# Sample state products of a hybrid decoder layer: high and low halves stacked on 128 rows in one fp32r matmul, in place of padded fp32

## The chip, the cores and the metric

The kernel runs on one core of one Trainium2 chip. The metric is the device time of one execution in microseconds (us). The engines are PE (TensorE: matmuls, and PEld, its weight loads), DVE (VectorE), ACT (ScalarE), POOL (GpSimd) and SP, which issues most of the DMAs.

## The reference, cut to what matters

One decoder layer serves 256 prompt tokens and a sample group of 8 sequences with 4 new tokens each (32 sample rows). Two recurrent branches update a 128x128 state for each sequence and head:

```python
# HGRN2, 16 heads
S = exp(G_last)[..., None] * S + einsum('bhsd,bhsv->bhdv', k * exp(G_last - G), i)
# gated delta rule, 32 value heads in 16 pairs
S = exp(g_last) * S + einsum('bhsd,bhsv->bhdv', k * exp(g_last - gam)[..., None], v_new)
```

The einsum over `s` (4 tokens for each sample sequence) is the "state product" that the change rewrites. Around it the layer does a large input projection, two output projections, a merge, and a feed-forward block.

## The kernel before

**Projections.** All dense products run on PE in `products` (L574 to L576). Weights arrive in pieces of 512 columns; ACT rounds each piece to fp32r (`whi`, L982), DVE takes the rest (`wlo`, L1429), and PE does three fp32r matmuls of 288 columns (256 prompt and 32 sample) for each 128-row block. A slab of 128 output columns is 48 such matmuls. Pieces are split three ahead of their use.

**Interleaving.** The recurrent work is written out by hand as steps `s` between the projection's matmuls: on PE there is a step before each 6 matmuls. An HGRN head spans 4 slabs (32 steps), a pair of delta heads 6 slabs (48 steps). Every engine walks the same step numbers in its own order and waits on counted semaphores; an engine that waits holds back all that stands behind it.

**HGRN state product of the sample** (head n). Step 0: PE transposes the 32 sample columns of decayed keys (`hX[:,3]`) and inputs (`hi_`) into bank 3 (L633, L634). Step 1: ACT copies them to `htoks` (L1070, semaphore `h_tok`); DVE masks scores into `hAT` (`h_at`). POOL then writes `hiX` (L2062, prompt) and `hiXs` (L2064): the 32 input rows repeated for 8 sequences and masked with `cm4`, 1024 columns (`h_spread`). Step 8: PE contracts `htok` with `hiX` (L643) and `htoks` with `hiXs` (L645), two 512-column matmuls each; rows 32 to 127 of the sample operands are zeros. Step 10: DVE adds the products to the states (L1574, L1578). Step 15: PE forms the outputs (L654 to L661).

**Delta state product of the sample** (pair n, e = 0, 1). Steps 42 to 44: PE transposes q, k, v (L707), ACT gets the norms, DVE scales q, k (`g_tokqk`) and v (L1704, `g_tokv`), then finishes the previous pair's output (L1792, L1794 `g_out`), which ACT rounds into `ohi` (L1243). POOL scales the keys by the decays (L2175: `gbek`, `gkl`, `gkls`), then issues the load of the next convolution rows (L2140). Step 0: PE transposes (L726), ACT copies (L1185 to L1190, `g_qpt`). Step 2: PE makes decay sums (L734, L735). Step 4: DVE makes `gA`, POOL the level masks (L2194), PE the halo transposes (L696); step 5: DVE does the gate product `gz` (L1721), the tap copies (L1656) and the halo copy (L1659); step 6: PE transposes level 0 (L753); step 7: DVE makes `gUi`, `gUs` (L1741, L1742); step 8: PE goes on (L765). Step 13: PE reads the old states; step 15: DVE makes `guTs`; step 16: PE transposes it; step 17: ACT copies `gvns` (L1216). POOL spreads it into `gvX` (L2225, once per e). Steps 20 and 24: PE contracts `gkls` with `gvX` (L817, two 512-column matmuls per step). Steps 21 and 25: DVE adds the product to the state (L1766).

## Time and profile before

| what | value |
|---|---|
| runs of the kernel before | 3898.64 us median of 3 (3895.19 to 3902.77) |
| profiled execution: its time | 3902.09 us |
| profiled execution: span, first to last instruction | 3900.6 us |
| PE busy | 3652.7 us (94%) |
| DVE, ACT, POOL busy | 2267.7, 1801.1, 869.9 us |
| mean granted TensorE clock | 0.956 of full speed |

A row of grouped instructions gives line, engine, operation, output and inputs, shapes and count, then busy us and mean ns of one. A matmul's modelled duration includes a tail that overlaps the next one, so the pace of PE is read from start to start. An fp32 matmul stands as two records.

### The profile page before, as it was taken

The numbers are of one execution on the slowest core, as the hardware profiler recorded it, in microseconds if no ns is written. First come the engines' busy times: TensorE is split into PE (matmuls) and PEld (weight loads), VectorE is DVE, ScalarE is ACT, GpSimd is POOL, SyncE is SP. The second block draws the span as 40 slices with busy tenths as digits, with TensorE's granted clock in tenths as the row PEclk, the third lists the DMA queues.
The fourth block names the chain that finished last, engine by engine and source line by source line (L and its number), as shares of the span: only waits on it lengthen the run. The fifth ranks groups of instructions, "written<-read, shape, count | busy, mean of one in ns | idle before, by whom it ended". The sixth has DMA issues, their size and how long they took to land.

```text
span 3900.6 us, 79284 instructions
## 1 busy us (share of the span) xinstructions
PE 3652.7 (94%) x25307; PEld 3326.0 (85%) x25307; DVE 2267.7 (58%) x4435; ACT 1801.1 (46%) x3802; POOL 869.9 (22%) x1035
## 2 busy tenths in 40 slices
PE   8799999999899999999999999999896999999997
PEld 1399999998888888888888988897685999999996
DVE  1466666646666656666566566545667545555555
ACT  1154544555454444445544454455463434444443
POOL 1022222211145444441244455411100000000000
PEclk9799999999999999999999999999997999999998
DMA  8454544568733333447634333357883555555553
GB/s 276 136 157 142 146 137 137 150 171 266 214 105 101 94 96 99 113 112 222 183 103 117 100 99 94 99 142 239 250 241 104 151 158 164 157 163 160 161 158 114
DMA packets 887591, 587.95 MB, mean 151 GB/s; under 512 B 23602, under 2 KB 820244, under 8 KB 886932
## 3 DMA queue, kind: packets, MB, share of 16 engines
q1 hardware_dynamic: 861268, 510.50, 45.6%
q0 software_dynamic: 26240, 76.41, 6.4%
q8 instruction: 43, 0.70, 0.1%
q14 instruction: 40, 0.33, 0.0%
...
## 4 chain that ended last, share of the span: by engine, by line
PE 80%; DVE 7%; issue 4%; ACT 3%; DMA 3%; POOL 1%; SPq 0%; DVEq 0%; ACTq 0%; POOLq 0%
PE acc L574 20%; PE acc L576 19%; PE acc L575 19%; PE acc L537 3%; PE bank L765 2%; PE bank L779 2%; PE bank L802 2%; PE bank L782 2%; PE bank L817 1%; DVE wlo L1429 1%; ACT whi L982 1%; PE bank L586 1%; DVE h_S L1574 1%; PE bank L587 1%; PE bank L661 1%
## 5 line engine op out<-in xcount | busy, mean ns | idle before, releaser
L1429 DVE TENSOR_TENSOR wlo<-raw,whi 128x512 fp32r<-128x512 f32 x1799 | 1266.5, 722 | 976.0 <-ACT whi L982 956.5
L982 ACT ACTIVATE whi<-raw 128x512 fp32r<-128x512 f32 x1799 | 1099.0, 628 | 992.4 <-PE acc L576 935.1
L574 PE MATMUL acc<-ahi,whi 128*128 128x288 f32 x4112 | 1305.2, 317 | 43.5 <-DVE wlo L1429 17.4
L575 PE MATMUL acc<-alo,whi 128*128 128x288 f32 x4112 | 1235.4, 300 | 0.0
L576 PE MATMUL acc<-ahi,wlo 128*128 128x288 f32 x4112 | 1231.1, 299 | 0.0
L574 PEld LDWEIGHTS acc<-ahi,whi 128*128 128x128 f32 x4112 | 793.9, 193 | 67.7 <-issue 41.0
L575 PEld LDWEIGHTS acc<-alo,whi 128*128 128x128 f32 x4112 | 795.4, 193 | 13.2 <-issue 11.5
L576 PEld LDWEIGHTS acc<-ahi,wlo 128*128 128x128 f32 x4112 | 795.1, 193 | 0.0
L574 PE MATMUL acc<-ohi,whi 128*128 128x288 f32 x1792 | 539.4, 301 | 26.1 <-DVE olo L1949 9.7
L575 PE MATMUL acc<-olo,whi 128*128 128x288 f32 x1792 | 534.0, 298 | 0.0
L576 PE MATMUL acc<-ohi,wlo 128*128 128x288 f32 x1792 | 532.3, 297 | 0.0
L574 PEld LDWEIGHTS acc<-ohi,whi 128*128 128x128 f32 x1792 | 340.9, 190 | 49.4 <-DVE wlo L1429 18.3
L575 PEld LDWEIGHTS acc<-olo,whi 128*128 128x128 f32 x1792 | 341.3, 190 | 2.4
L576 PEld LDWEIGHTS acc<-ohi,wlo 128*128 128x128 f32 x1792 | 342.3, 191 | 0.0
L1202 ACT ACTIVATE g_PU<-bank 128x512 f32<-128x512 f32 x80 | 47.8, 598 | 314.4 <-PE bank L765 239.2
L2194 POOL TENSOR_TENSOR g_lev<-g_A,levm 128x512 f32<-128x512 f32 x96 | 139.7, 1455 | 173.0 <-PE bank L765 114.4
L1752 DVE TENSOR_TENSOR g_Ui<-g_Ui,bank 128x512 f32<-128x512 f32 x80 | 54.7, 684 | 116.8 <-PE bank L782 111.6
L1672 DVE SCALAR_TENSOR_TENSOR g_ca<-g_U,g_cw,g_ca 128x312 f32<-128x312 f32 x192 | 118.0, 615 | 6.8
L537 PE MATMUL acc<-raw,cst 128*9 128x512 f32 x256 | 114.2, 601 | 8.0 <-DMA raw<-in_w_ada 8.0
L586 PE MATMUL bank<-whi,cs 128*18 128x512 f32 x256 | 101.3, 396 | 15.7 <-DVE wlo L1429 14.7
L765 PE MATMUL bank<-g_Ui,g_lev 128*128 128x128 f32 x640 | 88.1, 281 | 24.8 <-DVE g_Us L1742 22.1
L765 PEld LDWEIGHTS bank<-g_Ui,g_lev 128*128 128x128 f32 x640 | 78.7, 192 | 33.8 <-issue 33.7
...
## 6 DMA issues: line engine op xcount, KB each, us to landing
...
raw<-in_w_ada SPq DMA_DIRECT2D x192, 512.0 KB, 4.7
raw<-in_w_up SPq DMA_DIRECT2D x128, 512.0 KB, 4.1
raw<-in_w_down SPq DMA_DIRECT2D x128, 512.0 KB, 3.9
...
```

The costliest lines, as they stand in the source:

```text
L537: last = mm(acc[k][0:NC, :], cst[:, 2 * l + a, :], raw[:, 2 * (l % 4) + a].rearrange("p k c -> p (k c)"), start=(l + a == 0), stop=(l == 7 ...
L574: mm(bank[:, 0:T], whi[:, s, r, :], hi[:, kt, :], start=(kt == 0), stop=False, skip_group_check=True)
L575: mm(bank[:, 0:T], whi[:, s, r, :], lo[:, kt, :], start=False, stop=False, skip_group_check=True)
L576: last = mm(bank[:, 0:T], wlo[:, s, r, :], hi[:, kt, :], start=False, stop=(kt == KT - 1), skip_group_check=True)
L586: mm(R[4][0:2 * NC, :], cs2[:, kt, :], whi[:, s].rearrange("p k c -> p (k c)"), start=(kt == 0), stop=False)
L765: last = mm(R[3][:, p * P:(p + 1) * P], glev[:, l % 2, p, :], gUi[:, p, :], start=True, stop=True)
L779: last = mm(R[2][:, p * P:(p + 1) * P], gT[:, p, :], gPU[:, p, :], start=True, stop=True)
L782: last = mm(R[6][:, p * P:(p + 1) * P], gPU[:, p, :], gT[:, p, :], start=True, stop=True)
L982: f(whi[:, s], raw[:, r], ACT.Copy).then_inc(sg["hi_made"], 1)
L1429: tt_(wlo[:, s], raw[:, r], whi[:, s].bitcast(F32), SUB).then_inc(sg["lo_made"], 1)
L1672: stt(gca[:, 0:CW], gU[:, k, a:a + CW], gcw[:, k, a:a + 1], gca[:, 0:CW], MUL, ADD).then_inc(sg["g_part" if a < 3 else "g_tap"], 1)
L2194: last = pt(glev[:, l % 2], gA[:, :, :], levm[:, l, :].unsqueeze(1).to_broadcast([P, 4, P]), MUL)
```

## The change

The 32 sample rows of each state product are repeated four times along the partitions. One operand's four groups hold high, high, low, low (keys), the other's high, low, high, low (inputs or values), high being the fp32r rounding and low the rest. One fp32r matmul over 128 rows then sums all four cross products, in place of an fp32 matmul with 96 rows of zeros. To get there the transposes are fed with four copies (`hk4`, `hi4`, `gck4`, `guT4`), ACT rounds all rows, DVE overwrites the low groups with the difference, and POOL spreads 128 rows, with fp32r as output type. `gkls` leaves POOL; DVE makes `gk32` from bank 5 instead, and ACT and DVE split it at steps 4 and 5. Several of the new tiles lie in `gn1` and `gn2`, which are idle then. In the setup `cm4` becomes four stacked copies, and the strict mask of the sample is repeated for column 8 of `tab`.

```diff
-                htoks = sb("h_toks", [P, 2, P])
+                hvs = sb("h_vs", [P, P])
+                hst = sb("h_st", [P, 2, P], F32R)
+                hk4 = sb("h_k4", [P, 4, NS])
+                hi4 = sb("h_i4", [P, 4, NS])
                 hAT = sb("h_AT", [P, T])
                 hiX = sb("h_iX", [P, 2, 4, P])
-                hiXs = sb("h_iXs", [P, NB, P])
+                hiXs = sb("h_iXs", [P, NB, P], F32R)
...
-            gkls = sb("g_kls", [P, 2, P])
+            gkst = sb("g_kst", [P, 2, P], F32R)
...
+            gkhi = gn1[:, :, :].rearrange("p a t -> p (a t)")[:, 0:2 * P].rearrange("p (e d) -> p e d", d=P)
+            gvst = gn2[:, :, :].rearrange("p a t -> p (a t)")[:, 0:2 * P].rearrange("p (e v) -> p e v", v=P)
+            gck4 = gn2[:, :, :].rearrange("p a t -> p (a t)")[:, 2 * P:3 * P]
+            guT4 = gkhi.rearrange("p e (g b t) -> p e g b t", g=4, t=TS)
...
-                    turn(R[3][0:NS, 0:P], hX[:, 3, TP:T], ident[:, :])
-                    turn(R[3][0:NS, P:2 * P], hi_[:, TP:T], ident[:, :])
+                    turn(R[3][:, 0:P], hk4[:, :, :].rearrange("p g t -> p (g t)"), ident[:, :])
+                    turn(R[3][:, P:2 * P], hi4[:, :, :].rearrange("p g t -> p (g t)"), ident[:, :])
...
-                        last = mm(R[2 + a][:, :], htoks[:, 0, :], hiXs[:, 4 * a:4 * a + 4, :].rearrange("p c v -> p (c v)"),
+                        last = mm(R[2 + a][:, :], hst[:, 0, :], hiXs[:, 4 * a:4 * a + 4, :].rearrange("p c v -> p (c v)"),
...
-                    mm(R[7][:, TP:T], htoks[:, 1, :], hAT[:, TP:T], start=False, stop=False, skip_group_check=True)
+                    mm(R[7][:, TP:T], hvs[:, :], hAT[:, TP:T], start=False, stop=False, skip_group_check=True)
...
-                            last = turn(bank[0:m, k * P:(k + 1) * P], gC[:, k, a * P:a * P + m], ident[:, :])
+                            if (a, k) == (2, 1):
+                                turn(bank[:, k * P:(k + 1) * P], gck4, ident[:, :])
+                            else:
+                                last = turn(bank[0:m, k * P:(k + 1) * P], gC[:, k, a * P:a * P + m], ident[:, :])
...
-                        last = turn(R[5][0:NS, e * P:(e + 1) * P], guTs[:, e, :], ident[:, :])
+                        last = turn(R[5][:, e * P:(e + 1) * P], gkhi[:, e, :], ident[:, :])
...
                     pe.wait_ge(sg["g_vns"], n + 1)
+                    pe.wait_ge(sg["g_u1"], EARLIER + n + 1)
                     pe.wait_ge(sg["g_snew"], 2 * n + e)
                     for a in range(2):
-                        last = mm(R[4 + a][:, :], gkls[:, e, :], gvX[:, 4 * a:4 * a + 4, :].rearrange("p b v -> p (b v)"),
+                        last = mm(R[4 + a][:, :], gkst[:, e, :], gvX[:, 4 * a:4 * a + 4, :].rearrange("p b v -> p (b v)"),
...
                     act.wait_ge(sg["h_turned"], i)
+                    f(hi4[:, :, :], acc[at.bank(2)][:, TP:T].unsqueeze(1).to_broadcast([P, 4, NS]), ACT.Copy)
...
-                    f(htoks[0:NS, :, :], R[3][0:NS, 0:2 * P].rearrange("p (k d) -> p k d", d=P), ACT.Copy).then_inc(sg["h_tok"], 1)
+                    f(hvs[0:NS, :], R[3][0:NS, P:2 * P], ACT.Copy)
+                    f(hst[:, :, :], R[3][:, 0:2 * P].rearrange("p (k d) -> p k d", d=P), ACT.Copy).then_inc(sg["h_tok"], 1)
...
                 if s == 4:
+                    act.wait_ge(sg["g_tokv"], EARLIER + n + 1)
+                    f(gkhi[2 * NS:P].bitcast(F32R), gk32[2 * NS:P], ACT.Copy)
+                    f(gkst[0:2 * NS], gk32[0:2 * NS], ACT.Copy)
...
                     act.wait_ge(sg["g_vtt"], n + 1)
-                    f(gvns[0:NS, :, :], R[5][0:NS, 0:2 * P].rearrange("p (e v) -> p e v", v=P), ACT.Copy).then_inc(sg["g_vns"], 1)
+                    f(gvns[0:NS, :, :], R[5][0:NS, 0:2 * P].rearrange("p (e v) -> p e v", v=P), ACT.Copy)
+                    act.wait_ge(sg["g_olo"], n)
+                    f(gvst.bitcast(F32R), R[5][:, 0:2 * P].rearrange("p (e v) -> p e v", v=P), ACT.Copy).then_inc(sg["g_vns"], 1)
...
-                    tt_(hAT[0:NS, TP:T], R[4][0:NS, TP:T], smask[:, :], MUL).then_inc(sg["h_at"], 1)
+                    tt_(hAT[0:NS, TP:T], R[4][0:NS, TP:T], smask[:, :], MUL)
+                    dve.wait_ge(sg["h_tok"], n + 1)
+                    for rows_, k in ((slice(2 * NS, P), 0), (slice(NS, 2 * NS), 1), (slice(3 * NS, P), 1)):
+                        last = tt_(hst[rows_, k, :], R[3][rows_, k * P:(k + 1) * P], hst[rows_, k, :].bitcast(F32), SUB)
+                    last.then_inc(sg["h_at"], 1)
...
+                    if k == 1:
+                        tt_(gck4.rearrange("p (g b t) -> p g b t", g=4, t=TS),
+                            sample_of(gca[:, :], TS)[:, :, 0:TS].unsqueeze(1).to_broadcast([P, 4, NB, TS]),
+                            sample_of(gce[:, :], TS)[:, :, 0:TS].unsqueeze(1).to_broadcast([P, 4, NB, TS]), MUL)
...
-                            last = ts(gbv[0:m, a, e, :], bank[0:m, (2 + e) * P:(3 + e) * P], gsc[0:m, e, a:a + 1], None, MUL)
+                            ts(gbv[0:m, a, e, :], bank[0:m, (2 + e) * P:(3 + e) * P], gsc[0:m, e, a:a + 1], None, MUL)
+                    for e in range(2):
+                        last = ts(gk32[:, e, :], R[5][:, P:2 * P], gss[:, 2, 2, 1:2], gsc[:, e, 8:9], MUL, MUL)
...
+                    tt_(gkst[2 * NS:P], gk32[2 * NS:P], gkhi[2 * NS:P], SUB)
...
-                    tt_(guTs[:, :, :].rearrange("p e (b t) -> p e b t", t=TS), R[7][:, 64:128].rearrange("p (e b t) -> p e b t", e=2, t=TS),
-                        gqws[:, :, :, 1, :], ADD).then_inc(sg["g_vt"], 1)
+                    for e in range(2):
+                        last = tt_(guT4[:, e], R[7][:, 64 + e * NS:64 + (e + 1) * NS].rearrange("p (b t) -> p b t", t=TS).unsqueeze(1)
+                                   .to_broadcast([P, 4, NB, TS]), gqws[:, e, :, 1, :].unsqueeze(1).to_broadcast([P, 4, NB, TS]), ADD)
+                    last.then_inc(sg["g_vt"], 1)
+                if s == 17:
+                    dve.wait_ge(sg["g_vns"], n + 1)
+                    for rows_ in (slice(NS, 2 * NS), slice(3 * NS, P)):
+                        last = tt_(gvst[rows_], R[5][rows_, 0:2 * P].rearrange("p (e v) -> p e v", v=P), gvst[rows_], SUB)
+                    last.then_inc(sg["g_vlo"], 1)
...
-                pt(hiXs[0:NS, :, :], htoks[0:NS, 1, :].unsqueeze(1).to_broadcast([NS, NB, P]),
-                   cm4[:, :].unsqueeze(2).to_broadcast([NS, NB, P]), MUL).then_inc(sg["h_spread"], 1)
+                pool.wait_ge(sg["h_at"], n + 1)
+                pt(hiXs[:, :, :], hst[:, 1, :].bitcast(F32).unsqueeze(1).to_broadcast([P, NB, P]),
+                   cm4[:, :].unsqueeze(2).to_broadcast([P, NB, P]), MUL).then_inc(sg["h_spread"], 1)
...
-                pt(hX[:, 3, :], hk[:, :], hE[:, 3, :], MUL).then_inc(sg["h_decayed_p"], 1)
+                pt(hX[:, 3, :], hk[:, :], hE[:, 3, :], MUL)
+                pt(hk4[:, :, :], hk[:, TP:T].unsqueeze(1).to_broadcast([P, 4, NS]), hE[:, 3, TP:T].unsqueeze(1).to_broadcast([P, 4, NS]),
+                   MUL).then_inc(sg["h_decayed_p"], 1)
...
-                        scaled(gkl[:, a, c], P, a, 27 + 2 * a + c)
-                scaled(gkls[0:NS], NS, 2, 8).then_inc(sg["g_tokd"], 1)
+                        last = scaled(gkl[:, a, c], P, a, 27 + 2 * a + c)
+                last.then_inc(sg["g_tokd"], 1)
...
-                pool.wait_ge(sg["g_vns"], n + 1)
+                pool.wait_ge(sg["g_vlo"], EARLIER + n + 1)
...
-                    pt(gvX[0:NS, :, :], gvns[0:NS, e, :].unsqueeze(1).to_broadcast([NS, NB, P]),
-                       cm4[:, :].unsqueeze(2).to_broadcast([NS, NB, P]), MUL).then_inc(sg["g_vx"], 1)
+                    pt(gvX[:, :, :], gvst[:, e, :].unsqueeze(1).to_broadcast([P, NB, P]),
+                       cm4[:, :].unsqueeze(2).to_broadcast([P, NB, P]), MUL).then_inc(sg["g_vx"], 1)
```

## Rows read from the trace of the kernel before

**Rows 1.** The page: its header, busy time of PE, chain that ended last.

```profile
span 3900.6 us, 79284 instructions
PE 3652.7 (94%) x25307; PEld 3326.0 (85%) x25307; DVE 2267.7 (58%) x4435; ACT 1801.1 (46%) x3802; POOL 869.9 (22%) x1035
...
PE 80%; DVE 7%; issue 4%; ACT 3%; DMA 3%; POOL 1%; SPq 0%; DVEq 0%; ACTq 0%; POOLq 0%
```

**Rows 2.** Groups of instructions on PE, whole span.

```profile
L586 PE MATMUL bank<-whi,cs 128*18 128x512 f32 x256 | 101.3, 396 | 15.7 <-DVE wlo L1429 14.7
...
L817 PE MATMUL bank<-g_vX,g_kls 128*128 128x512 f32 x128 | 60.2, 592 | 0.0
...
L645 PE MATMUL bank<-h_iXs,h_toks 128*128 128x512 f32 x64 | 30.1, 592 | 0.0
```

**Rows 3.** Timeline of PE, HGRN step 8: start us, duration us, instruction.

```profile
222.10 1.88 PE L643 MATMUL bank<-h_iX,h_tok 128*128 128x512 f32 x4
223.82 1.88 PE L645 MATMUL bank<-h_iXs,h_toks 128*128 128x512 f32 x4
...
226.20 0.30 PE L576 MATMUL acc<-ahi,wlo 128*128 128x288 f32 x1
226.33 0.29 PE L574 MATMUL acc<-ahi,whi 128*128 128x288 f32 x1
```

**Rows 4.** Timeline of PE, HGRN step 0: transposes of 128 and 32 columns.

```profile
214.56 0.27 PE L632 MATMUL bank<-ident,h_i 128*128 128x128 f32 x1
214.66 0.27 PE L633 MATMUL bank<-ident,h_X 128*32 128x128 f32 x1
214.77 0.27 PE L634 MATMUL bank<-ident,h_i 128*32 128x128 f32 x1
```

**Rows 5.** Waits of PE, 1000 to 2740 us: total us, times, longest.

```profile
PE bank L765 <- DVE g_Us L1742: 22.1, 14, 3.1
PE bank L696 <- DMA g_cc<-in_cache_conv: 19.7, 13, 1.7
PE bank L734 <- ACT g_QW L1190: 12.2, 15, 1.2
```

**Rows 6.** Timeline of ACT and POOL, HGRN steps 1 to 8.

```profile
216.78 0.36 ACT L1070 ACTIVATE h_toks<-bank 32x256 f32<-32x256 f32 x1
...
219.22 2.34 POOL L2064 TENSOR_TENSOR h_iXs<-h_toks,cm 32x1024 f32<-32x1024 f32 x1
```

**Rows 7.** Groups on POOL, 1125 to 1750 us.

```profile
L2219 POOL TENSOR_TENSOR g_S<-g_S,g_sc 128x1024 f32<-128x1024 f32 x14 | 26.2, 1888 | 4.3 <-PE bank L802 3.8
```

**Rows 8.** Single HGRN heads (first three) and delta pairs: window, length, busy, PEclk.

```profile
223.82:261.04 37.22, 36.78 (x252) 34.37 (x251) 24.56 (x49) 18.09 (x39) 8.80 (x8) 0.95 0.50 144
...
410.00:446.00 36.00, 35.48 (x252) 32.87 (x251) 23.82 (x49) 18.05 (x38) 8.79 (x8) 1.00 0.51 148
...
705.50:744.30 38.80, 38.28 (x251) 35.88 (x250) 23.88 (x49) 18.14 (x37) 8.79 (x8) 0.91 0.47 137
...
1136.10:1222.10 86.00, 81.11 (x595) 75.75 (x594) 54.05 (x112) 40.15 (x101) 40.46 (x45) 0.96 0.37 101
...
1563.50:1646.50 83.00, 78.20 (x595) 72.63 (x594) 53.71 (x112) 40.20 (x101) 40.36 (x45) 1.00 0.38 104
```

**Rows 9.** Timelines of DVE, ACT and PE, delta step 44 to step 2.

```profile
1249.76 1.62 DVE L1704 TENSOR_SCALAR g_bv<-bank,g_sc 128x128 f32<-128x128 f32 x6
...
1252.74 1.06 DVE L1794 TENSOR_TENSOR g_n<-g_o,g_z 128x576 f32<-128x576 f32 x1
...
1253.93 0.69 ACT L1243 ACTIVATE ohi<-g_n 128x576 f32 x1
...
1256.62 0.70 PE L734 MATMUL bank<-g_GR,m_incl 128*128 128x256 f32 x2 [0.83 <-ACT g_QW L1190]
```

**Rows 10.** Timelines of POOL and DVE, delta steps 4 and 5.

```profile
1262.18 2.47 POOL L2194 TENSOR_TENSOR g_lev<-g_A,levm 128x512 f32<-128x512 f32 x1 [2.90 <-DVE g_As L1732]
...
1263.04 0.44 DVE L1721 TENSOR_TENSOR g_z<-g_ca,g_ce 128x288 f32<-128x288 f32 x1
1263.40 4.32 DVE L1656 COPY g_cw<-vec 128x4 f32 x3
```

**Rows 11.** Timelines of POOL and PE, delta steps 17 to 20.

```profile
1292.54 2.01 POOL L2225 TENSOR_TENSOR g_vX<-g_vns,cm 32x1024 f32<-32x1024 f32 x1 [0.90 <-ACT g_vns L1216]
...
1299.05 1.45 PE L817 MATMUL bank<-g_vX,g_kls 128*128 128x512 f32 x3
```

More of the change, by code:

```diff
@@ L234, in hybrid_layer @@
             cm32 = sb("cm32", [P, P // HC])
+            cm4w = sb("cm4w", [P, 4 * NB])
+            mstr4 = sb("mstr4", [NS, P])
             lbt = sb("lbt", [P, HH, 2])
@@ L315, in hybrid_layer @@
                 gto = scoped(rows_out)("g_to", [27, 4, P])
-            gvX = sb("g_vX", [P, NB, P])
+                gk32 = scoped(rows_out)("g_k32", [P, 2, P])
+            gvX = sb("g_vX", [P, NB, P], F32R)
             gS = sb("g_S", [P, 4, 2, P])
@@ L1016, in _ @@
             f(bgs[:, 0:128], R[5][:, 0:128], ACT.Exp)
-            f(bgs[0:NS, 128:192], R[5][0:NS, 128:192], ACT.Exp)
+            f(bgs[0:NS, 128:160], R[5][0:NS, 128:160], ACT.Exp)
+            f(bgs[:, 160:192], R[5][:, 160:192], ACT.Exp)
             f(bgs[:, 192:576], R[3][:, 0:384], ACT.Exp).then_inc(sg["chunk_exp"], 1)
@@ L1487, in _ @@
             for b in range(NB):
-                last = ts(gxs[:, b, :], bgT[0:NS, 2, GH:2 * GH], cm4[:, b:b + 1], None, MUL)
+                last = ts(gxs[:, b, :], bgT[0:NS, 2, GH:2 * GH], cm4[0:NS, b:b + 1], None, MUL)
+            last = copy(mstr4[:, :].rearrange("p (g t) -> p g t", t=NS), m_str_s[:, :].unsqueeze(1).to_broadcast([NS, 4, NS]))
             last.then_inc(sg["bg_taken"], 1)
@@ L1497, in _ @@
                 for k in range(2):
-                    copy(tab[0:m, :, 3 + 3 * k + a], sums[:, k])
+                    copy(tab[0:m, :, 3 + 3 * k + a], sums[:, k]) if (a, k) != (2, 1) else copy(tab[:, :, 8], bgs[:, 160:192])
                 for c in range(2 if a < 2 else 0):
@@ L1504, in _ @@
             for rows_ in (slice(NS, 2 * NS), slice(2 * NS, P)):
-                nc.vector.memset(hiXs[rows_, :, :], 0.0)
                 nc.vector.memset(hAT[rows_, TP:T], 0.0)
-                last = nc.vector.memset(htoks[rows_, :, :], 0.0)
+                last = nc.vector.memset(hvs[rows_, :], 0.0)
             last.then_inc(sg["tab_made"], 1)
@@ L1634, in _ @@
             for rows_ in (slice(NS, 2 * NS), slice(2 * NS, P)):
-                nc.vector.memset(gvX[rows_, :, :], 0.0)
-                nc.vector.memset(gkls[rows_, :, :], 0.0)
                 nc.vector.memset(gvns[rows_, :, :], 0.0)
@@ L2017, in _ @@
                                     pattern=[[-1, P]], channel_multiplier=1).then_inc(sg["consts_made"], 1)
-            for t in (hmask, smask, reset, cm32, cm4, cm64, m_incl, m_str, m_str_s):
+            for t in (hmask, smask, reset, cm32, cm4w, cm64, m_incl, m_str, m_str_s):
                 nc.gpsimd.memset(t[:, :], 1.0)
@@ L2031, in _ @@
                 keep(chunked(t, n_, m), [[m, n_], [0, m]], m - 1, -1)
-            for t, n_, m in ((cm32, P // HC, HC), (cm4, NB, TS), (cm64, 2, GC)):
+            for t, n_, m in ((cm32, P // HC, HC), (cm4w, 4 * NB, TS), (cm64, 2, GC)):
                 keep(t[:, :], [[-m, n_]], 0, 1)
                 keep(t[:, :], [[m, n_]], m - 1, -1)
+            ADD = ALU.add
+            step(pt(cm4w[:, 0:2 * NB], cm4w[:, 0:2 * NB], cm4w[:, 2 * NB:4 * NB], ADD))
+            step(pt(cm4[:, :], cm4w[:, 0:NB], cm4w[:, NB:2 * NB], ADD))
             for l in range(LEV):
```

9 lines of the change are left out of this document (4 added, 5 removed).

## The prediction

> **What bounds the kernel now.** I read the page's header first: PE is busy for 3652.7 of 3900.6 us, and the chain that ended last is 80% PE [rows 1]. So time taken off PE's queue counts in full, unless a wait opens in its place. The groups of PE come next, for what the change replaces: L817 and L645 are 128 and 64 records, that is 64 and 32 fp32 matmuls of 512 columns [rows 2]. They run at full clock (592 ns modelled everywhere). The timeline gives their real pace: four records of L643 start at 222.10, those of L645 at 223.82, so two fp32 matmuls take 1.72 us and one takes 0.86 us [rows 3]. Third, PE's waits in the delta stages, since these show which other engines hold PE up: 22.1 us on DVE's `gUs`, 19.7 us on the convolution rows' DMA, 12.2 us on ACT's `gQW` [rows 5]. Nothing waits at L645 or L817. Fourth, the lengths of single heads beside the clock: an HGRN head takes 37.2 us, a delta pair 83 to 86 us [rows 8]. Last, the engines' timelines around each new instruction.
>
> **Removed from PE.** The 96 fp32 matmuls become 96 fp32r ones. No fp32r matmul with 128 stationary and 512 moving columns stands in the trace. Lower bound: fp32r products of 288 columns start 0.13 us apart [rows 3], so by columns 512 cost 0.13 x 512/288 = 0.24 us. Upper bound: L586, fp32r with 512 columns, has a modelled duration of 0.396 us [rows 2], tail included. The same tail is in the product's 0.29 against its pace of 0.13 (0.16), and 0.396 - 0.16 = 0.24 again. I take 0.24. The saving is 96 x (0.86 - 0.24) = 59.5 us, of which 19.8 in the HGRN heads (1.24 each) and 39.7 in the delta pairs (2.48 each). With 0.396 it would be 44.5 us.
>
> **Wider transposes.** Two per HGRN head and three per delta pair, 80 in all, go from 32 to 128 stationary columns. Transposes of both widths start 0.10 to 0.11 us apart [rows 4], so I take zero. A rule speaks against that: the Trainium skill ("TensorE: Matmul & The Clock Gate", section on LDWEIGHTS) has the load's time grow with the columns, columns/1.2 ns; by it 96 more columns cost an estimated 0.08 us, 6.4 us over all if none of it were hidden. The starts agree with a load hidden behind the stream of the identity.
>
> **HGRN, between steps 1 and 8.** ACT's one copy of 32x256 becomes two, so `h_tok` comes about 0.2 us later (a copy's issue distance in this stretch; bounds 0 and a whole copy, 0.36 [rows 6]). DVE takes three differences from bank 3 before `h_at`; POOL's new wait for `h_at` falls while `hiX` is being written, which keeps it covered. `hiXs` now covers 128 rows; rows count for nothing on POOL, since 128x1024 takes 1.888 us [rows 7] and the 32x1024 `gvX` takes 2.01 [rows 11]. `hiXs` ended at 219.22 + 2.34 = 221.56, and PE's step 8 began at 222.10 [rows 3, 6]: slack 0.5 us, against 0.2 plus some contention of POOL with DVE. I take 0.1 us of new wait in 16 heads: +1.6 us (bounds 0 and 0.5 x 16 = 8). What stands behind the step on DVE is the next `wlo`, three pieces ahead of PE. The extra POOL product `hk4` and ACT copy `hi4` have whole steps of PE's work before their readers: zero; without that cover they would cost their own length, some 0.4 us each per head.
>
> **Delta pairs, step 44 to step 2.** DVE gets two more scalings (`gk32`) right behind L1704. Six of those take 1.62 us, so two take 0.5 us [rows 9]. DVE is busy without a gap from there to `g_out` (L1794 ends at 1253.80), ACT's L1243 starts at 1253.93 behind it, then come the copies up to L1190, and PE waits 0.83 us for these at L734 [rows 9]. Nothing on this chain has slack, so PE's step 2 is 0.5 us later in 15 pairs: +7.5 us (bounds 0, should ACT's own work be the later one, and 7.5). Removing `gkls` from POOL brings the convolution rows' DMA forward, and part of L696's 19.7 us wait goes [rows 5]. It gains nothing: PE gets to step 6 earlier only to wait for POOL's level 0, and to step 8 to wait for DVE's `gUs`.
>
> **Delta pairs, steps 4 to 8.** ACT's two copies at step 4 fit before DVE needs the gate. DVE's new difference of 64x256 at step 5 costs what L1721 does by size, 0.44 x 256/288 = 0.38 us. It stands on the chain to `gUs`: the three tap copies behind it take 4.32 us and end only when POOL's run of products pauses [rows 10], and PE waits at L765 for what follows. So 0.38 x 15 = +5.7 us. Upper bound: the difference is held for one POOL instruction. L2194 took 2.47 us, about 1.3 of it while DVE was at work; the rest is what one such product takes alone, some 1.2 us; that price gives 1.2 x 15 = 18 us. The row shows POOL giving way: L1721 kept its 0.44 us while L2194 ran [rows 10]. The Trainium skill ("SBUF — State Buffer", section "SBUF: two separate sides") has an exclusive lock here for a DVE operation with two SBUF inputs against POOL, held for the whole instruction. By that rule the loser may as well be the DVE difference, and the sum would be nearer the upper bound.
>
> **Delta pairs, steps 15 to 20.** `guT4` is two sums for one (+0.2 us). ACT's `gvst`, then DVE's two differences behind its step 17 work, make POOL's first `gvX` start at about 1295.9 in place of 1292.54. It then ends near 1297.9, before PE's 1299.05 [rows 11]: 1.1 us of slack stays, zero cost. The second `gvX` starts from the first L817, which moves with it: zero. The setup gets a few small instructions: +0.5 us.
>
> **Sum.** -59.5 + 1.6 + 7.5 + 5.7 + 0.5 = -44.2 us. The profiled execution took 3902.09 us for a span of 3900.6 us; it lies 3.5 us above the median of the runs, 3898.64. I subtract from the median: 3854 us.
>
> **The clock.** It is not in the sum and carries much of the range. A head with clock 1.00 takes 36.0 us, with 0.95 37.2, with 0.91 38.8; a pair takes 83.0 at 1.00 and 86.0 at 0.96 [rows 8]. These are stretches at 1.2 in place of 2.4 GHz around waits and short matmuls. Shorter heads place them anew. If no HGRN head had one I estimate -19 us (1.2 in some 14 heads, more in two), if all had two +23; the pairs could give the same again, either way. I take half of one of these, 20 us, as what may come.
>
> **Rivals.**
> *Contention.* `hiXs` later by 0.5 us (POOL and DVE hinder each other) and the step 5 difference held for a POOL product: 8 in place of 1.6, 18 in place of 5.7. Sum -44.2 + 6.4 + 12.3 = -25.5, 3873 us. For it: `hiXs` took 2.34 us against 1.888 for the same columns elsewhere. Against: L1721 was not held. 16 in 100.
> *The clock gives back.* Fewer half-clock stretches since waits and dense work fall otherwise: another -20, 3834 us. For it: the 36.0 us heads exist. Against: the short matmuls of step 15 stay. 13 in 100.
> *Slower.* POOL writes fp32r in no row; only DVE and ACT do. If its products with fp32r output were much longer, by x us each, PE would wait x - 0.2 in 16 heads and x - 1.1 in 16 pairs (x - 2.8 more at the second). The gain is gone at 32x = 65, x = 2.0: products of 3.9 us, twice today's. Three times today's, x = 3.8, gives +117 - 44 = +73, 3972 us. Against: nothing hints that an output type has a price. 5 in 100.
> *The change doesn't do what it says, or gains nothing.* Four passes all the same, or weight supply sets the pace: 3899 us. Against: L586's 0.396 us for 512 columns, and DMA at half load with DVE at 24.6 of 37.2 us [rows 2, 8]. 3 in 100.
> *Forecast.* 3854 us, its own range 3838 to 3868: 63 in 100.
>
> **How the numbers follow.** The likeliest case gives 3854. Forecast, clock rival and most of contention span 3828 to 3880; outside lie the slower and empty cases (8) and the tails of the clock and of contention (12). What can't be told from no change is 0.2%, 7.8 us. Faster: 63 + 13 + 15 of contention = 91. Same: 3 + 1 of contention = 4. Slower: 5.
>
> **What would show it.** L817 and L645 as 64 and 32 records with starts 0.24 us apart; HGRN heads of about 36.0 us at clock 0.95 and 34.8 at 1.00; pairs about 1.6 us shorter; waits at L734 and L765 longer by 7.5 and unchanged, with a new wait for level 0 at L753; the wait for the DMA at L696 shorter. It is wrong if L643 waits for POOL over 0.5 us in each head, if POOL's `hiXs` or `gvX` is over 2.5 us, or if the mean clock moves from 0.956 by over 0.01.

## The result: slower, and the profile after

The changed kernel takes 3945.49 us in the median of 4 runs (3940.86 to 3955.11), the kernel before 3900.22 us beside it (3895.19 to 3902.77). The ratio is 1.0123 with a 95% interval of 1.0103 to 1.0144: about 45 us slower, where 44 us faster was forecast. The profiled execution has a span of 3939.4 us, 38.8 us more than before, and a mean granted clock of 0.944 (0.956 before).

The page of the changed kernel, header, PE's row and the chain that ended last (to be set beside [rows 1]):

```profile
span 3939.4 us, 79330 instructions
PE 3632.2 (92%) x25211; PEld 3343.5 (85%) x25211; DVE 2372.3 (60%) x4590; ACT 1822.6 (46%) x3883; POOL 864.6 (22%) x1037
...
PE 76%; DVE 12%; issue 5%; ACT 4%; DMA 3%; DVEq 1%; SPq 0%; POOL 0%; ACTq 0%; POOLq 0%
```

PE's busy time fell by only 20.5 us, and its idle time rose from 247.9 us (3900.6 - 3652.7) to 307.2: +59.3. The two make the +38.8. On the chain DVE went from 7% to 12%.

The products that replace them, as groups and in the timelines of a head and a pair (beside [rows 2, 3, 11]):

```profile
L830 PE MATMUL bank<-g_vX,g_kst 128*128 128x512 f32 x64 | 21.4, 415 | 0.0
L654 PE MATMUL bank<-h_iXs,h_st 128*128 128x512 f32 x32 | 16.4, 595 | 0.0
```

```profile
223.47 1.88 PE L652 MATMUL bank<-h_iX,h_tok 128*128 128x512 f32 x4
224.79 1.02 PE L654 MATMUL bank<-h_iXs,h_st 128*128 128x512 f32 x2
225.65 0.29 PE L583 MATMUL acc<-ahi,whi 128*128 128x288 f32 x1
...
1306.34 0.63 PE L830 MATMUL bank<-g_vX,g_kst 128*128 128x512 f32 x2
1306.81 0.29 PE L583 MATMUL acc<-ahi,whi 128*128 128x288 f32 x1
```

96 records stand where 192 stood. Two products of L830 end 0.47 us after they start (1306.34 to 1306.81), so one takes 0.235 us; in the head all four take 2.18 us, of which the two fp32 ones have 1.72 by [rows 3] and the two new ones 0.46. The 0.24 us of the forecast was right, and so were its 59.5 us.

PE's waits between 1000 and 2740 us (beside [rows 5]; total us, times, longest):

```profile
PE bank L777 <- DVE g_Us L1772: 71.7, 15, 4.8
PE bank L746 <- ACT g_QW L1206: 21.1, 15, 1.9
PE bank L765 <- POOL g_levs L2239: 16.7, 16, 3.8
PE bank L777 <- DVE g_Ui L1782: 15.1, 16, 2.7
```

Before, the same stretch had 22.1 us for `g_Us` and 12.2 for `g_QW` [rows 5]. The same view of before also has the first line below; the second is its group of L765, with the idle time ahead of it, by releaser, at the end:

```profile
PE bank L753 <- POOL g_levs L2196: 6.6, 2, 4.2
```

```profile
L765 PE MATMUL bank<-g_Ui,g_lev 128*128 128x128 f32 x640 | 88.1, 281 | 24.8 <-DVE g_Us L1742 22.1 <-DVE g_Ui L1752 0.4
```

So `g_Us` costs +49.6, `g_Ui` +14.7, `g_levs` +10.1, `g_QW` +8.9, and the wait for the convolution rows' DMA (19.7) is gone: +63.6 us. Smaller waits of this stretch give 5.9 back (wlo 8.8 to 5.0, `g_ss` 9.0 to 6.3, `olo` 6.0 to 6.6). So the waits of the delta stages cover the +59.3 of idle time. This is the first half of the answer.

The second half is the clock. A mean of 0.944 over 3939.4 us, between full and half speed, means (1 - 0.944) x 2 x 3939.4 = 441 us at 1.2 GHz; before it was 0.044 x 2 x 3900.6 = 343. PE's busy time shows what the 98 us cost: -59.5 + x = -20.5 gives x = 39 us. This is a remainder: it would also hold any cost of the wider transposes, but those still start 0.11 us apart.

Single HGRN heads and one delta pair (beside [rows 8]; the columns are as there):

```profile
224.80:260.70 35.90, 35.46 (x250) 33.94 (x249) 25.62 (x53) 18.37 (x40) 9.67 (x9) 0.95 0.54 149
298.40:336.10 37.70, 37.18 (x250) 35.59 (x249) 25.54 (x53) 18.35 (x40) 9.66 (x9) 0.91 0.50 141
524.70:559.50 34.80, 34.27 (x249) 32.49 (x248) 25.45 (x53) 18.21 (x40) 9.65 (x9) 1.00 0.54 153
1433.60:1522.20 88.60, 79.97 (x590) 76.08 (x589) 58.45 (x117) 41.29 (x105) 39.02 (x44) 0.94 0.36 97
```

At each clock a head is 1.1 to 1.3 us shorter than before, as forecast: 34.8 for 36.0, 35.9 for 37.2, 37.7 for 38.8. But of the 15 heads that can be measured from one state product to the next, 11 are now of the 0.91 kind, against two before. Fifteen heads, from the first one's step 15 on, before and after:

```profile
230.80:790.20 559.40, 551.67 (x3752) 515.12 (x3751) 358.97 (x734) 271.52 (x556) 131.81 (x120) 0.95 0.49 143
```

```profile
231.80:788.40 556.60, 548.70 (x3720) 524.48 (x3721) 382.74 (x779) 275.01 (x585) 144.93 (x135) 0.93 0.51 143
```

Of 15 x 1.24 = 18.6 us only 2.8 arrived. The delta pairs took 83 to 86 us before and take 88 to 89 now.

**Where the 4.8 us per pair come from.** Timelines of DVE and POOL in the window that [rows 10] show for before:

```profile
1259.58 0.39 DVE L1761 SCALAR_TENSOR_TENSOR g_As<-g_GRs,g_sc,bank 32x32 f32<-32x32 f32 x2
...
1260.39 1.58 DVE L1450 TENSOR_TENSOR wlo<-raw,whi 128x512 fp32r<-128x512 f32 x1
1261.89 3.33 DVE L1750 TENSOR_TENSOR g_z<-g_ca,g_ce 128x288 f32<-128x288 f32 x1
1265.26 0.43 DVE L1768 TENSOR_TENSOR g_kst<-g_k,g_n 64x256 fp32r<-64x256 f32 x1
1265.70 1.82 DVE L1679 COPY g_cw<-vec 128x4 f32 x3
...
1269.24 0.20 DVE L1772 TENSOR_TENSOR g_Us<-ident,bank 32x64 f32<-32x64 f32 x1
```

```profile
1260.13 1.29 POOL L2237 TENSOR_TENSOR g_lev<-g_A,levm 128x512 f32<-128x512 f32 x1 [4.56 <-DVE g_As L1761]
...
1262.12 1.26 POOL L2237 TENSOR_TENSOR g_lev<-g_A,levm 128x512 f32<-128x512 f32 x1
...
1263.62 1.28 POOL L2247 TENSOR_TENSOR g_T<-ident,g_lev 128x512 f32<-128x512 f32 x1
...
1265.47 1.33 POOL L2237 TENSOR_TENSOR g_lev<-g_A,levm 128x512 f32<-128x512 f32 x1
```

```profile
1269.59 2.04 PE L777 MATMUL bank<-g_Ui,g_lev 128*128 128x128 f32 x8 [4.78 <-DVE g_Us L1772]
```

And in the kernel before, the two ends of the same stretch of DVE and what PE did behind it:

```profile
1261.63 0.39 DVE L1732 SCALAR_TENSOR_TENSOR g_As<-g_GRs,g_sc,bank 32x32 f32<-32x32 f32 x2
...
1269.01 0.20 DVE L1742 TENSOR_TENSOR g_Us<-ident,bank 32x64 f32<-32x64 f32 x1
```

```profile
1269.35 1.13 PE L765 MATMUL bank<-g_Ui,g_lev 128*128 128x128 f32 x8 [1.76 <-DVE g_Us L1742]
```

In before POOL's first product was the one stretched (2.47 us) while DVE's gate product took 0.44 [rows 10]. Now it is the other way round: the product takes 1.29 us, the conversion ahead of the gate product 1.58 us and the gate product 3.33 us. The gate product ends at 1265.22, behind POOL's `g_T` (1264.90). The gate product takes 3.3 us in 15 of 16 pairs; before it did so in 2 of 16. The gate product is an old instruction in an old place; the change doesn't touch it. PE idles 4.78 us, and its next eight matmuls run at half speed (2.04 us; the same eight took 1.13 in a pair of before).

DVE was held in the kernel before too, only elsewhere: its three tap copies took 4.32 us [rows 10], and 0.42 where nothing holds them (`difference_last` below). So not all of the 3.33 us is new. From the end of `g_As` to the end of `g_Us` DVE took 7.2 us before and takes 9.5 now, 2.3 us more. PE, for its part, is ready for `g_Us` 4.8 us after `g_As` in place of 5.6: its DMA wait of 1.43 us in this pair is gone, and 0.88 at POOL's levels has come. The two make the 3.0 us between 1.76 and 4.78.

### The profile page after: what moved, and what is told of

The parts are those of the page before. It is cut to its first block, busy times and chain, and to the rows that moved or that the text cites. A ratio compares the mean times of both kernels' runs of the same rounds, so it can differ in the third digit from the quotient of the medians.

```text
span 3939.4 us, 79330 instructions
## 1 busy us (share of the span) xinstructions
PE 3632.2 (92%) x25211; PEld 3343.5 (85%) x25211; DVE 2372.3 (60%) x4590; ACT 1822.6 (46%) x3883; POOL 864.6 (22%) x1037
## 4 chain that ended last, share of the span: by engine, by line
PE 76%; DVE 12%; issue 5%; ACT 4%; DMA 3%; DVEq 1%; SPq 0%; POOL 0%; ACTq 0%; POOLq 0%
PE acc L583 19%; PE acc L585 18%; PE acc L584 18%; PE acc L546 3%; PE bank L777 2%; PE bank L791 2%; DVE g_z L1750 2%; PE bank L814 1%; DVE wlo L1450 1%; PE bank L794 1%; DMA raw<-in_w_ada 1%; ACT whi L995 1%; PE bank L670 1%; PE bank L595 1%; DVE g_ca L1695 1%
## 5 line engine op out<-in xcount | busy, mean ns | idle before, releaser
L1450 DVE TENSOR_TENSOR wlo<-raw,whi 128x512 fp32r<-128x512 f32 x1799 | 1291.5, 737 | 927.3 <-ACT whi L995 912.1
L2237 POOL TENSOR_TENSOR g_lev<-g_A,levm 128x512 f32<-128x512 f32 x96 | 124.6, 1298 | 276.0 <-PE bank L777 146.2
L777 PE MATMUL bank<-g_Ui,g_lev 128*128 128x128 f32 x640 | 102.6, 310 | 88.9 <-DVE g_Us L1772 71.7
L777 PEld LDWEIGHTS bank<-g_Ui,g_lev 128*128 128x128 f32 x640 | 89.9, 216 | 101.4 <-issue 101.2
L1695 DVE SCALAR_TENSOR_TENSOR g_ca<-g_U,g_cw,g_ca 128x312 f32<-128x312 f32 x192 | 137.8, 718 | 6.8
L595 PE MATMUL bank<-whi,cs 128*18 128x512 f32 x256 | 101.6, 397 | 15.1 <-DVE wlo L1450 14.1
```

Of the source, the lines that this page charges most:

```text
L595: mm(R[4][0:2 * NC, :], cs2[:, kt, :], whi[:, s].rearrange("p k c -> p (k c)"), start=(kt == 0), stop=False)
L777: last = mm(R[3][:, p * P:(p + 1) * P], glev[:, l % 2, p, :], gUi[:, p, :], start=True, stop=True)
L1450: tt_(wlo[:, s], raw[:, r], whi[:, s].bitcast(F32), SUB).then_inc(sg["lo_made"], 1)
L1695: stt(gca[:, 0:CW], gU[:, k, a:a + CW], gcw[:, k, a:a + 1], gca[:, 0:CW], MUL, ADD).then_inc(sg["g_part" if a < 3 else "g_tap"], 1)
L2237: last = pt(glev[:, l % 2], gA[:, :, :], levm[:, l, :].unsqueeze(1).to_broadcast([P, 4, P]), MUL)
```

## The experiments

Each has its ratio to the kernel before, run on the same chip, with the 95% interval. Spans and waits are those of its profiled execution.

**One part alone.** `hgrn_only` has the change in the HGRN heads only, `gdn_only` in the delta pairs only.

```diff
+                hst = sb("h_st", [P, 2, P], F32R)          # hgrn_only
+                hiXs = sb("h_iXs", [P, NB, P], F32R)
...
+            gkst = sb("g_kst", [P, 2, P], F32R)            # gdn_only
+            gvX = sb("g_vX", [P, NB, P], F32R)
```

> Only the HGRN heads carry the change; the delta pairs are as before. Theory 1 (the loss lies in the delta pairs, where POOL and DVE contend at step 4; in the HGRN heads the matmul's gain is nearly all lost to a second half-clock stretch): heads of 37.7 us at clock 0.91 and of 34.8 at 1.00 as in the changed kernel, the whole 2 to 5 us under the kernel before. Rival (the HGRN part has its share in the loss): 10 us or more above the kernel before.

> Only the delta pairs carry the change; the HGRN heads are as before. Theory 1: all of the loss and a little more, 46 to 52 us above the kernel before, with the gate product on DVE at 3.3 us and PE's wait for gUs at about 70 us in total. Rival: 35 us or less above it.

Measured: `hgrn_only` 3899.81 us, 1.0000 (0.9987 to 1.0013). `gdn_only` 3950.33 us, 1.0131 (1.0114 to 1.0149). PE waits 71.8 us for `g_Us` in it, 21.0 for `g_QW`, 16.7 for `g_levs` and 15.1 for `g_Ui`.

The whole loss is in the pairs, with the same waits as in the full change, as the first theory of `gdn_only` had it. The HGRN part gains nothing measurable: the 2 to 5 us that I expected of it did not show, and the interval leaves room for them.

**Where the HGRN gain went.** `hgrn_filler` is `hgrn_only` with five more fp32r products of 512 columns in each head, whose result nobody reads: 16 x 5 x 0.24 = 19 us of PE work, as much as the change took away.

```diff
                     last.then_inc(sg["h_ds"], 1)
+                    for _ in range(5):
+                        mm(R[4][:, :], hst[:, 0, :], hiXs[:, 0:4, :].rearrange("p c v -> p (c v)"), start=True, stop=True)
```

> Only the HGRN part of the change, and behind it in each head five more fp32r matmuls of 512 columns into bank 4, which nothing reads: 1.2 us of PE work per head, 19 us in all, which gives the head its old length. Theory 3 (the matmul's gain in the HGRN heads went to half-clock stretches, whose number per head goes with the head's length and place): heads of 36.0 us at clock 1.00 and 37.2 at 0.95 again, the whole within 5 us of the run without the five matmuls (3900 us). Rival (the gain was lost in a wait): 14 us or more above it.

Measured: 3900.34 us, 1.0007 (0.9992 to 1.0022). Against the kernel before beside it that is 3.0 us more, where `hgrn_only` is 0.3 us less: 19 us of work cost about 3 us, with an uncertainty of some 8. The same fifteen heads, in `hgrn_only` and in `hgrn_filler`:

```profile
230.80:783.10 552.30, 544.44 (x3721) 519.98 (x3721) 382.56 (x779) 275.42 (x585) 144.91 (x135) 0.94 0.51 144
```

```profile
233.80:793.20 559.40, 551.54 (x3795) 524.04 (x3796) 382.60 (x779) 274.95 (x585) 145.01 (x135) 0.95 0.51 143
```

18 us of added work made the fifteen heads 7.1 us longer. (The profiled execution of `hgrn_only` is its fastest, 3888.25 us against a median of 3899.81, so these heads are shorter than in most of its runs.) The other 11 us were paid back by the clock: the heads are again 36.0, 37.2 and 38.8 us long, and two of them have the 0.91, against nine in that execution of `hgrn_only`. So PE's work in this stage is traded against half-speed stretches. Why a head 1.2 us shorter falls into two of them more often is open.

**Undoing the hold.** `gate_first` is the changed kernel, with POOL's level 0 waiting until the gate product is written.

```diff
                 if l == 0:
                     pool.wait_ge(sg["g_a"], EARLIER + n + 1)
+                    pool.wait_ge(sg["g_z"], 2 * n + 2)
```

> The changed kernel, and POOL's level 0 also waits for DVE's gate product of step 5 (g_z), so that the two-input work of DVE is over before POOL begins. Theory 1 (DVE's gate product, held for 3.3 us behind POOL's run of products, makes gUs late): the gate product back at 0.44 us, PE's wait for gUs from 71.7 down to about 35 us although POOL starts later, the whole 3900 to 3918 us. Rival (the work added to DVE and ACT makes gUs late, not its contention): no faster than the changed kernel, 3943 to 3960 us, since a wait was added.

Measured: 3917.89 us, 1.0036 (1.0017 to 1.0054), 28 us less than the change by the medians. PE's waits:

```profile
PE bank L765 <- POOL g_levs L2240: 34.6, 16, 4.5
PE bank L777 <- DVE g_Us L1772: 23.0, 15, 1.8
```

The gate product takes 0.44 us again and the wait for `g_Us` is 48.7 us shorter (I had expected 35 us to be left; 23.0 are); POOL starts its levels later, which gives 17.9 us back. The tap copies are held for 4.18 us again, as before, so `g_As` to `g_Us` still takes 7.6 us. Keeping the gate product out of POOL's run gives back 28 of the 45 us: its hold is shown to be a large part of the loss.

**Which instruction is held.** `difference_last` moves only the new difference (L1768) behind `gUs`; `gate_last` moves only the gate product there and leaves the difference, behind the same wait on ACT that the gate product had.

```diff
                 if s == 5:
                     silu_z(2 * n + 2, 1)                                               # moved in gate_last
                     tt_(gkst[2 * NS:P], gk32[2 * NS:P], gkhi[2 * NS:P], SUB)           # moved in difference_last
...
                 if s == 7:
                     (gUi, gUs)
+                    (the moved line)
```

> The changed kernel with only the new difference of 64x256 (L1768) moved behind gUi and gUs at step 7; the gate product g_z stays where it was. It tests my own term (the difference costs its 0.38 us on the chain, up to 1.2 if held). Theory A (what is held is the gate product, as the first DVE operation with two SBUF inputs behind the conversion; the difference costs its own 0.42 us only): g_z still 3.33 us, the wait at g_Us about 65 us, 3939 us (3932 to 3948). Theory B (the difference's being there is what sets DVE against POOL's run): g_z back at 0.44 us, the wait at g_Us at 22 us, 3895 to 3905 us.

> The counterpart: the gate product g_z moved behind gUi and gUs at step 7, the new difference L1768 stays at step 5, behind the same wait on ACT as before. Theory A (whichever DVE operation with two SBUF inputs comes first behind the conversion is held until POOL's run of products pauses, whatever it is): the difference takes 3.3 us in 15 pairs, the wait at g_Us about 65 us, 3939 us (3930 to 3948). Theory B (it is the gate product's own matter, its size or place, and a smaller operation slips in): the difference takes about 0.42 us, gA's end to gUs's end about 6 to 7 us, the wait at g_Us 15 us or less, 3885 to 3898 us.

Measured: `difference_last` 3914.67 us, 1.0041 (1.0025 to 1.0056); `gate_last` 3915.07 us, 1.0040 (1.0025 to 1.0054). DVE in `difference_last`, then in `gate_last`:

```profile
1256.94 3.33 DVE L1750 TENSOR_TENSOR g_z<-g_ca,g_ce 128x288 f32<-128x288 f32 x1
1260.19 0.42 DVE L1679 COPY g_cw<-vec 128x4 f32 x3
```

```profile
1262.09 3.20 DVE L1768 TENSOR_TENSOR g_kst<-g_k,g_n 64x256 fp32r<-64x256 f32 x1
```

Whichever of the two stands first behind the conversion is held: the gate product for 3.33 us, or the difference, a 0.43 us instruction, for 3.20 (in 14 pairs; in one DVE went first and it took 1.39). On this, theory A of both expectations is right. On the time both my numbers (3939) were wrong by 24 us. The second instruction of the two costs far more than its 0.43 us: with both in place the tap copies start at 1265.70, behind the start of POOL's next product at 1265.47, and take 1.82 us; with one of them they start ahead of that product and take 0.42 us (0.34 in `gate_last`). From the end of `g_As` to that of `g_Us` it is 9.5 us with both, 8.0 with either. The wait for `g_Us` falls from 71.7 us to 50.3 and 50.0, and the time by 31 us.

**Why POOL wins now.** Two ideas, both tried. The first: the conversion meets POOL some 0.1 us later or earlier. `before_dup` is the kernel before with its last mask product in two halves, which delays the conversion by 0.07 us.

```diff
-                    tt_(gQKms[:, :], R[5][0:NS, 160:192], smask[:, :], MUL).then_inc(sg["g_qkm"], 1)
+                    tt_(gQKms[:, 0:16], R[5][0:NS, 160:176], smask[:, 0:16], MUL)
+                    tt_(gQKms[:, 16:32], R[5][0:NS, 176:192], smask[:, 16:32], MUL).then_inc(sg["g_qkm"], 1)
```

> The kernel before, and DVE's last small product of step 4 (gQKms) in two halves, so that the wlo behind it starts 0.1 us later against POOL's level 0. Theory 1 (who begins first is decided within some 0.1 us): POOL goes first in all pairs, the gate product takes 3.3 us in place of 0.44, gUs comes 0.8 to 0.9 us later and the time is 10 to 30 us above the kernel before. Rival (the time follows the work added): 1 to 2 us above it, the gate product still at 0.44 us in 14 pairs of 16.

Measured: 3902.4 us, 1.0000 (0.9990 to 1.0010); the gate product is held in the same 2 pairs of 16, the wait for `g_Us` 21.1 us. The idea fell, as far as a delay of this size goes.

The second: it is what POOL did before. The change takes the `gkls` scaling off POOL. `keys_on_dve` is the kernel before with that scaling made on DVE; `pool_product_kept` is the changed kernel with a scaling of that size kept on POOL, into a tile that is overwritten later.

```diff
+                    for e in range(2):                                        # keys_on_dve, DVE step 44
+                        last = ts(gkls[0:NS, e, :], R[5][0:NS, P:2 * P], gss[0:NS, 2, 2, 1:2], gsc[0:NS, e, 8:9], MUL, MUL)
-                scaled(gkls[0:NS], NS, 2, 8).then_inc(sg["g_tokd"], 1)        # and off POOL
...
+                scaled(gPU[0:NS, 0:2, :], NS, 2, 8).then_inc(sg["g_tokd"], 1) # pool_product_kept, on POOL
```

> The kernel before with one edit: the product gkls, POOL's last before it issues the convolution rows' DMA, is made on DVE from bank 5 (two scalings behind those of gbv), and POOL's is dropped. Theory 2 (what POOL did before its wait for level 0 decides who goes first; dropping gkls lets POOL win): the gate product at 3.3 us in all pairs, gUs 0.8 us or more later, the whole 3918 to 3935 us. Rival (only the two scalings cost): the gate product stays at 0.44 us, PE waits 0.5 us longer for gQW, the whole 3903 to 3912 us.

> The changed kernel with one edit: POOL makes a product of 32x256 in the place where gkls stood (into gPU, where nothing reads it). Theory 2: the gate product is back at 0.44 us in most pairs and PE's wait for gUs falls to 25 to 40 us in total, the whole 3905 to 3920 us. Rival (something else in the change decides who goes first): the gate product stays at 3.3 us, the whole 3940 to 3952 us.

Measured: `pool_product_kept` 3949.57 us, 1.0126 (1.0098 to 1.0155), with 71.5 us at `g_Us`: the product on POOL brings nothing back. `keys_on_dve` 3931.7 us, 1.0085 (1.0054 to 1.0116). It waits 33.3 us for `g_levs`, 28.0 for `g_QW` and 13.5 for `g_Us`, the last in 4 pairs only. Its gate products in two successive pairs:

```profile
1089.02 3.34 DVE L1723 TENSOR_TENSOR g_z<-g_ca,g_ce 128x288 f32<-128x288 f32 x1
1175.69 0.44 DVE L1723 TENSOR_TENSOR g_z<-g_ca,g_ce 128x288 f32<-128x288 f32 x1
```

The time was in the expected range, but by another road. The hold comes in 4 pairs, not in all, so the second idea fell as it was put. PE's wait at `g_QW` grows by 15.8 us and that at the levels by 26.7, while those for the convolution rows (19.7) and `g_Us` (8.6) shrink: +14 us. PE's busy time is 16.0 us longer (3668.7 for 3652.7), at a clock of 0.949 for 0.956. So this edit, which takes work off POOL and puts two instructions on DVE, costs 33 us alone. What decides between DVE and POOL is not settled. POOL's first product starts 0.26 us ahead of the conversion in most pairs of before, where it loses, and of the changed kernel, where it wins; in `keys_on_dve`, with the same 0.26, it wins in 2 pairs and loses in 11. So the starts in the records don't tell who goes first.

**Taking the contest away.** `dve_reordered` is the changed kernel with DVE's order in the pairs changed: tap copies at step 3, `gUi` and `gUs` at step 6 ahead of that step's conversion, gate product and difference behind them.

```diff
-                if s == 5:
+                if s == 3:
                     (tap copies)
+                if s == 5:
                     (halo copy)
-                if s == 5:
-                    silu_z(2 * n + 2, 1)
-                    tt_(gkst[2 * NS:P], gk32[2 * NS:P], gkhi[2 * NS:P], SUB)
-                if s == 7:
+                if s == 6:
                     (gUi, gUs)
+                if s == 7:
+                    silu_z(2 * n + 2, 1)
+                    tt_(gkst[2 * NS:P], gk32[2 * NS:P], gkhi[2 * NS:P], SUB)
```

`before_reordered` is its control: the same order in the kernel before.

> The changed kernel with DVE's order changed in the delta pairs: the tap copies at step 3 in place of 5 (DVE idles there), gUi and gUs before the wlo of step 6, the gate product and the difference of gkst behind them. Theory 1 (the loss is DVE work held behind POOL's run on the way to gUs): PE's wait for gUs falls from 71.7 us to under 15 in total, the whole 3865 to 3890 us, under both kernels. Rival (the added work itself, or the clock, makes the loss): over 3920 us.

> The kernel before, with the order of DVE's work in the delta pairs that dve_reordered has: tap copies at step 3, gUi and gUs at step 6 ahead of that step's conversion, the gate product behind them at step 7. It is the control for the 3847.9 us of dve_reordered. Theory 1 (the change is worth its 40 us of matmuls in the pairs once the hold is gone, and the reorder alone removes only before's own g_Us wait of 22.1 us and the stretching of the level products): 3870 to 3885 us, the wait at g_Us gone, so the change on top of the reorder is worth 20 to 35 us. Rival theory (all of dve_reordered's gain is the reorder, and the change is worth nothing even then): 3845 to 3852 us. Rival theory 3 (before's order was as good for before, the reorder only repairs the changed kernel): 3895 to 3902 us.

Measured: `dve_reordered` 3847.87 us (3840.25 to 3850.93), 0.9855 (0.9826 to 0.9883): faster than both kernels, about 100 us faster than the changed one, and 17 us below the range that I expected. The kernel before took 3897.38 us beside it, so the gain is 50 us by the medians and 56 by the ratio. `before_reordered` 3876.85 us, 0.9940 (0.9921 to 0.9958). DVE in `dve_reordered`, and PE's waits in it:

```profile
1249.11 0.67 DVE L1450 TENSOR_TENSOR wlo<-raw,whi 128x512 fp32r<-128x512 f32 x1
...
1252.09 0.69 DVE L1769 TENSOR_TENSOR g_Ui<-ident,bank 128x512 f32<-128x512 f32 x1 [2.14 <-PE bank L767]
...
1252.82 1.68 DVE L1450 TENSOR_TENSOR wlo<-raw,whi 128x512 fp32r<-128x512 f32 x1
```

```profile
PE bank L765 <- POOL g_levs L2240: 24.6, 16, 3.4
PE bank L746 <- ACT g_QW L1206: 21.2, 15, 1.9
```

DVE now waits for PE ahead of `gUi`, not PE for DVE, and the wait for `g_Us` is gone. The conversion behind is still held (1.68 us), where nobody waits for it. The first conversion takes 0.67 us again, in 15 of 16 pairs: in this order DVE also goes first, which was not planned and is not explained. The reorder alone is worth 22 us, as much as before lost at `g_Us`. The change on top of it is worth 0.9855 / 0.9940 = 0.9914, some 33 us, or 29 by the medians; 20 to 35 were expected. The two profiled executions differ by 26.7 us of span: 1.4 in the fifteen heads, so almost nothing is kept of the HGRN part, and 24 in the pairs. There 39.7 us of matmuls are saved and the convolution rows' wait of 20.4 us goes, while the waits grow by 9.0 at `g_QW`, 15.1 at `g_Ui` and 19.2 at the levels. That makes -17; the other 7 us are not accounted for.

**The term for the scalings.** `scalings_late` is `dve_reordered` with the two `gk32` scalings behind `g_out`.

```diff
                 if s == 46:
                     dve.wait_ge(sg["g_out"], EARLIER + j)
+                    for e in range(2):
+                        last = ts(gk32[:, e, :], R[5][:, P:2 * P], gss[:, 2, 2, 1:2], gsc[:, e, 8:9], MUL, MUL)
+                    last.then_inc(sg["g_tokv"], 1)
                     silu_z(2 * j + 1, 0)
```

> dve_reordered with one more move: the two new key scalings g_k32 go behind g_out on DVE (step 46), so that the chain g_out, ACT's casts and copies, g_QW, PE's step 2 starts 0.5 us earlier, and bank 5 comes free for the last transposes of step 0 later, about 1240.8 in place of 1238.6, while ACT does not read their result before 1241.6. Theory 1 (my term of 0.5 us in 15 pairs for the scalings is what the g_QW wait grew by): the wait at g_QW falls from 21.2 us to 12 to 15 us and the time to 3838 to 3843 us. Rival theory (ACT's own queue or the late transposes set that wait, and the scalings cost nothing there): the wait stays at 19 us or more, or moves to L738 or L746 behind g_tokv, 3846 to 3852 us.

Measured: 3863.19 us (3854.91 to 3873.98), 0.9895 (0.9874 to 0.9916), slower than `dve_reordered` by 15 us, or by 10 when each is set against the kernel before beside it; that the move gains nothing is clear, the size of the loss is not. The wait at `g_QW` is gone altogether, and this stands in its place. Below it are two pairs of `scalings_late` and one of `dve_reordered`:

```profile
PE bank L738 <- DVE g_k L1744: 23.1, 15, 1.6
```

```profile
1334.90:1417.80 82.90, 78.35 (x591) 74.90 (x590) 55.17 (x117) 41.37 (x105) 39.70 (x44) 0.96 0.38 103
1417.80:1502.30 84.50, 80.01 (x591) 76.59 (x590) 55.19 (x117) 41.35 (x105) 39.74 (x44) 0.94 0.38 103
```

```profile
1328.40:1409.90 81.50, 77.09 (x590) 73.54 (x589) 55.11 (x117) 41.37 (x105) 39.81 (x44) 0.98 0.39 106
```

The waits are alike (23.1 for 21.2); PE's busy time in these pairs is 1.3 and 2.9 us longer at a lower clock. These are not all pairs: in `dve_reordered` most take 81.5 us and some 83.1, in `scalings_late` most take 83.1 or 84.2, on average 1.4 us more. Over the span PE's busy time is 22.0 us longer and its idle time 1.1, in an execution that is the slowest of its four. The rival theory was right that the wait moves, and neither theory had the price. That the moved wait of 1.6 us set off further half-speed stretches is read from these rows; no run isolates it.

## Why the prediction was wrong

**The step that failed: "Delta pairs, steps 4 to 8", +5.7 us with an upper bound of 18.** It priced the new difference and took its 0.44 us neighbour for settled. Two things were wrong. The difference pushes the tap copies behind POOL's next product, so it costs 1.5 us on the chain: 21.4 us of waiting, 31 us of time (`difference_last`). And the contest that the row showed DVE winning turned round: the gate product is held for 3.33 us in 15 pairs (`gate_first`: 28 us back when it isn't). The two overlap and don't add up: the stretch from `g_As` to `g_Us` grew by 2.3 us, where the term had 0.38. The contention rival named this place and this mechanism, but the wrong instruction, and sized it by one POOL product where the hold lasted over several; the tap copies' 4.32 us in its own row were already such a hold. Its 19 us beyond the forecast were far too small. Why POOL wins in the changed kernel stays open. The Trainium skill ("SBUF — State Buffer", section "SBUF: two separate sides") has the pair of ports as an exclusive lock for a DVE operation with two SBUF inputs against POOL; the traces agree (3.33 and 3.20 us for operations of 0.44), and the prediction weighed it against one pair in which DVE won; in two other pairs of that trace the gate product took 3.3 us. The same section of the Trainium skill also gives the pair of ports to whichever starts first. The records as they stand don't bear that out: POOL's product starts 0.26 us ahead in both kernels, and is the one stretched in the kernel before.

**"The clock", ±20 us and not in the sum.** It took some 39 us of PE's busy time. It was counted as a spread about zero, of half of one stage's swing; it went one way in both stages. In HGRN it took 15.8 of the 18.6 us of the fifteen heads, and `hgrn_filler` shows the trade from the other side. In the pairs each of the 15 waits of 4.7 to 4.8 us for `g_Us` is followed by matmuls at half speed, and none of the waits of 0.2 to 3.1 us in before is. (The estimate of -19 us for heads without half speed comes out with the 11 heads of 37.2 us that the trace has, not with the 14 that it names.) The sign named for it, a mean clock off 0.956 by over 0.01, came true.

**"Delta pairs, steps 15 to 20", zero.** Also wrong, by 14.7 us. L830 does not wait for POOL, as worked out, but `gvX` now runs at 1297.19 to 1299.13 instead of 1292.54, and DVE's tap products meet it there. The changed kernel, DVE and PE, then DVE before:

```profile
1297.41 3.22 DVE L1695 SCALAR_TENSOR_TENSOR g_ca<-g_U,g_cw,g_ca 128x312 f32<-128x312 f32 x3
...
1301.26 0.69 DVE L1782 TENSOR_TENSOR g_Ui<-g_Ui,bank 128x512 f32<-128x512 f32 x1
```

```profile
1302.10 1.13 PE L777 MATMUL bank<-g_Ui,g_lev 128*128 128x128 f32 x8 [0.73 <-DVE g_Ui L1782]
```

```profile
1295.49 1.70 DVE L1672 SCALAR_TENSOR_TENSOR g_ca<-g_U,g_cw,g_ca 128x312 f32<-128x312 f32 x3
...
1299.25 0.69 DVE L1752 TENSOR_TENSOR g_Ui<-g_Ui,bank 128x512 f32<-128x512 f32 x1 [1.46 <-PE bank L782]
```

Before, this update of `gUi` ended at 1299.94, 1.6 us ahead of PE's use of it at 1301.56. The products that stood between were shortened from 1.72 to 0.5 us, and DVE, held up at the taps (3.22 us for 1.70), is late with the update: together they open the wait. No run isolates it: it is read from the trace.

**What held.** The price of the products (0.235 us for 0.24) and with it the 59.5 us. The `gQW` chain: +8.9 for +7.5, though `scalings_late` shows that it can't be bought back by moving the scalings. No wait at the head's step 8, as L652 shows none; heads 1.2 us shorter at equal clock. No price for POOL's fp32r output: a `gvX` with little in its way takes 1.90 us for 1.89. So the rival called slower was right only in that the kernel got slower; its cause did not occur. `hiXs` takes 2.35 us in all 16 heads, but the 2.34 of [rows 6] was not the usual value: before it took 2.34 in 3 heads and 1.89 in 13, in which the `hiX` ahead of it was the stretched one (1.49 for 1.04). The transfer of the convolution rows: its wait went (19.7 us) and 10.1 came back at POOL's level 0.

Summed against the span: -59.5 for the matmuls, +63.6 for waits, +39 for the clock make +43, against a measured +38.8; the smaller waits (-5.9) account for the difference to within 2 us. The 39 is itself the remainder of the busy time, so this sum tests the waits, not the clock.
